# Where the taps of a 31-wide depthwise convolution add up: SBUF tiles or one PSUM bank

## What is computed

```python
z = u @ w_in                                   # q, six k/v sets, gates, conv input, merge gates
kc = compress(kv[0], ...); vc = compress(kv[1], ...)
#   compress: 31 overlapping windows of 32 tokens -> gelu(flat @ w1) @ w2
o_c, o_s, o_w = nsa_attention(q, kc, vc, ...)  # 8 heads of 64, query blocks of 128

c = c_val * sigmoid(c_gate)                    # 512 channels
c = causal_dwconv(c, conv_w, conv_b)           # 31 taps per channel, 512 tokens
c = silu(layernorm(c)) ; y_b = c @ w_conv_out + b
h = h + (sigmoid(..) * y_a + sigmoid(..) * y_b) @ w_out
```

## Time and profile before

| | |
|---|---|
| median of three runs | 2301.78 us |
| profiled execution | 2300.76 us, of which the span of the trace is 2298.8 us |
| TensorE matmul busy | 2156.7 us (94%) |
| VectorE busy | 1082.4 us (47%) |
| ScalarE busy | 863.0 us (38%) |
| GpSimd busy | 925.4 us (40%), 855.4 of it `w_lo` |
| mean granted TensorE clock | 0.973 of full speed |
| the tap instruction, SBUF accumulator | 90 times, 104.0 us |
| the tap instruction, PSUM accumulator | 29 times, 21.7 us |

### The profile page before, as it was taken

One profiled execution on the slowest core, in us unless ns is written; L12 is line 12 of the kernel. 1 busy time (PEld: TensorE's weight loads), 2 busy tenths in 40 slices (PEclk: granted clock), 3 DMA queues, 4 the chain that ended last, 5 costly groups with the idle time before them and its releaser, 6 DMA issues.

```text
span 2298.8 us, 25188 instructions
## 1 busy us (share of the span) xinstructions
PE 2156.7 (94%) x10138; PEld 1766.7 (77%) x10138; DVE 1082.4 (47%) x1665; ACT 863.0 (38%) x1344; POOL 925.4 (40%) x415
## 2 busy tenths in 40 slices
PE   7449999999999999989999999999899999999996
PEld 6437777778888888777777888888788788888875
DVE  3996666535552423556654423222553245222145
ACT  4123444434442335444443423223532234233243
POOL 4242222344444444522215444443654454444452
PEclk9779999999999999999999999999999999999998
DMA  4122111223333233211112233232223223333321
GB/s 151 55 92 65 47 45 48 73 92 102 101 92 101 93 105 105 64 56 56 46 37 93 92 101 101 92 101 92 93 71 103 90 75 101 93 100 97 96 90 49
DMA packets 53252, 192.73 MB, mean 84 GB/s; under 512 B 5904, under 2 KB 6032, under 8 KB 53136
## 3 DMA queue, kind: packets, MB, share of 16 engines
q1 hardware_dynamic: 52704, 189.55, 26.4%
q10 hardware_dynamic: 432, 1.57, 0.2%
HBM read 189.00 MB, written 2.10 MB: 83 GB/s over the span
## 4 chain that ended last, share of the span: by engine, by line
PE 82%; DVE 12%; ACT 5%; issue 1%; POOL 0%; DMA 0%; DVEq 0%; ACTq 0%; POOLq 0%
PE ps L461 25%; PE ps L463 24%; PE ps L462 24%; DVE conv_acc L1044 4%; PE ps L625 1%; PE ps L605 1%; PE ps L864 1%; ACT w_hi L1646 1%; DVE ps L1553 1%; PE ps L617 1%; PE ps L524 1%; PE ps L882 1%; DVE resid L1558 1%; DVE tile_a L1312 1%; PE ps L517 1%
## 5 line engine op out<-in xcount | busy, mean ns | idle before, releaser
L425 POOL TENSOR_TENSOR w_lo<-w_raw,w_hi 128x1024 fp32r<-128x1024 f32 x353 | 855.4, 2425 | 1303.8 <-ACT w_hi L1646 1303.8
L461 PE MATMUL ps<-xg_hi,w_hi 128*128 128x512 f32 x1776 | 712.1, 401 | 38.1 <-POOL w_lo L425 17.1
L463 PE MATMUL ps<-xg_hi,w_lo 128*128 128x512 f32 x1776 | 697.2, 393 | 0.0
L462 PE MATMUL ps<-xg_lo,w_hi 128*128 128x512 f32 x1776 | 697.0, 392 | 0.0
L1646 ACT ACTIVATE w_hi<-w_raw 128x1024 fp32r<-128x1024 f32 x353 | 372.7, 1057 | 623.6 <-PE ps L463 615.0
L461 PEld LDWEIGHTS ps<-xg_hi,w_hi 128*128 128x128 f32 x1776 | 336.8, 190 | 107.6 <-issue 22.2
L463 PEld LDWEIGHTS ps<-xg_hi,w_lo 128*128 128x128 f32 x1776 | 336.2, 189 | 71.7
L462 PEld LDWEIGHTS ps<-xg_lo,w_hi 128*128 128x128 f32 x1776 | 337.2, 190 | 63.9 <-issue 0.2
L462 PE MATMUL ps<-h_lo,w_hi 128*128 128x512 f32 x688 | 267.9, 389 | 0.0
L463 PE MATMUL ps<-h_hi,w_lo 128*128 128x512 f32 x688 | 267.9, 389 | 0.0
L461 PE MATMUL ps<-h_hi,w_hi 128*128 128x512 f32 x688 | 267.9, 389 | 0.0
(11 more groups left out here) (303 smaller groups left out, 2335.2 us busy)
## 6 DMA issues: line engine op xcount, KB each, us to landing
w_raw<-in_weights SPq DMA_DIRECT2D x353, 512.0 KB, 3.5
resid<-in_x SPq DMA_DIRECT2D x4, 512.0 KB, 6.9
out_x<-resid SPq DMA_DIRECT2D x8, 256.0 KB, 2.0
p_raw<-in_p ACTq DMA_DIRECT2D x3, 512.0 KB, 3.6
vec<-in_vectors SPq DMA_DIRECT2D x1, 252.5 KB, 4.3
```

Of the source, the lines that this page charges most:

```text
L425: pool.tensor_tensor(w_lo[:, slot, :], w_raw[:, u % RAW, :], w_hi[:, slot, :].bitcast(F32), ALU.subtract).then_inc(w_ready, 1)
L461: pe.matmul(o, w, x, start=start, stop=False)
L462: pe.matmul(o, w, xl, start=False, stop=False)
L463: return pe.matmul(o, wl, x, start=False, stop=stop)
```

## The change

All four channel tiles now add up in bank 7, one after the other; the last tap of each writes the finished sum to `conv_acc[:, ct, :]`, as tile 3's did. Since the next tile's first tap overwrites the bank, it waits for the last tap of the tile before it. Bank 7 is therefore taken from the first tap on, and both kinds of compressed features are turned into bank 6: kind 0 into columns 0 to 127, kind 1 into columns 128 to 255. TensorE may not write kind 1 while VectorE or ScalarE still read kind 0 there, so `hidden_turn(1)` waits for `hidden_low(0)`.

```diff
             def hidden_turn(kv):
                 pe.wait_ge(s_cmp["gelu"], kv + 1)
+                if kv:
+                    pe.wait_ge(s_cmp["glo"], 1)
                 for half in range(2):
-                    mm = pe.transpose(ps[:, 6 + kv, half * 64:half * 64 + 2 * NC1], ...)
+                    mm = pe.transpose(ps[:, 6, kv * P + half * 64:kv * P + half * 64 + 2 * NC1], ...)
...
                     ct, k = divmod(n, CONV_TAPS)
-                    acc, src, w = conv_acc[:, ct, :], glu[:, ct, k:k + S], vcol("conv_w", n)
-                    if ct == CT - 1:
-                        acc = ps[:, NB, :]
+                    acc, src, w = ps[:, NB, :], glu[:, ct, k:k + S], vcol("conv_w", n)
                     if k == 0:
+                        if n:
+                            dve.wait_ge(s_mrg["conv"], n)
                         ins = dve.tensor_scalar(acc, src, w, vcol("conv_b", ct), ALU.mult, ALU.add)
```

More of the change, by code:

```diff
@@ L550, in hidden_turn @@
                 pe.wait_ge(s_cmp["gelu"], kv + 1)
+                if kv:
+                    pe.wait_ge(s_cmp["glo"], 1)
                 for half in range(2):
-                    mm = pe.transpose(ps[:, 6 + kv, half * 64:half * 64 + 2 * NC1], hid[:, kv, half * P:(half + 1) * P],
+                    mm = pe.transpose(ps[:, 6, kv * P + half * 64:kv * P + half * 64 + 2 * NC1], hid[:, kv, half * P:(half + 1) * P],
                                       ident[0:2 * NC1, 0:2 * NC1])
@@ L1088, in hidden_low @@
                 dve.wait_ge(s_cmp["ghi"], kv + 1)
-                low(hid_lo[:, kv], ps[:, 6 + kv, 0:P].rearrange("p (a b) -> p a b", b=64)[:, :, 0:2 * NC1], hid_hi[:, kv],
+                low(hid_lo[:, kv], ps[:, 6, kv * P:(kv + 1) * P].rearrange("p (a b) -> p a b", b=64)[:, :, 0:2 * NC1], hid_hi[:, kv],
                     s_cmp["glo"])
@@ L1710, in hidden_high @@
                 act.wait_ge(s_cmp["turned"], kv + 1)
-                copy_hi(hid_hi[:, kv], ps[:, 6 + kv, 0:P].rearrange("p (a b) -> p a b", b=64)[:, :, 0:2 * NC1], s_cmp["ghi"])
+                copy_hi(hid_hi[:, kv], ps[:, 6, kv * P:(kv + 1) * P].rearrange("p (a b) -> p a b", b=64)[:, :, 0:2 * NC1], s_cmp["ghi"])
             def keys(j):
```

## The result

| | before | after |
|---|---|---|
| median | 2301.82 us (4 runs, 2301.23 to 2309.78) | 2274.28 us (4 runs, 2272.36 to 2276.49) |
| profiled execution | 2300.76 us | 2272.36 us |
| its span | 2298.8 us | 2270.6 us |

The ratio is 0.9873, 95% interval 0.9849 to 0.9896. The kernel is 27.5 us faster; 33.0 were forecast (2268.8 us, range 2264 to 2275). The time is inside the range, near its slow end.

What follows compares the result with a forecast made beforehand. VectorE's taps were taken to bound the kernel from 52.3 to 170.3 us, TensorE after that. VectorE's 32.5 us plus 0.5 us from TensorE's clock made 33.0 us, so 2301.8 becomes 2268.8 us, range 2264 to 2275.

Steps and rivals of the forecast that it cites:

- A: Dependent taps in PSUM are slower than isolated ones, up to 21 us over 80 taps: 2272 to 2290 us; 4%.
- B: Compression chain becomes the bound at `hidden_low(0)`, `values` 0 comes 3 to 7 us later: 2272 to 2276 us; 5%.
- the cycle table: 120 fixed cycles for a PSUM source, 58 for SBUF: 65 ns more a tap, 5.2 us over 80, 2274 us.
- The stall: Taps with one PSUM operand no longer wait for `w_lo`: 16 long taps on the path save 32.3 us.
- The sum of VectorE's stretch: From 52.3 to 170.3 us VectorE saves 32.5 us, so `values` 0 starts at about 137.8.
- First taps: Three on the path become 804 ns: one saves 0.7 us, two cost 0.26 us each; together 0.2 us saved.
- Spacing in PSUM: Dependent taps keep SBUF's 0.787 us; bounds 0.01 us less a tap and 0.04 us more (3.2 us).
- D: Each tap reads back the PSUM value just written; at 0.5 us extra a tap, 2308.8 us; 2%.
- The slack list: Competitors for the path stay early enough: 2.3 us of slack at `hidden_low(0)`, 6 us at `keys` 1.
- The new wait: `hidden_turn(1)` waits for `hidden_low(0)`, asked for at 118.5, TensorE there at 123 to 125 us: costs nothing.
- TensorE's clock: Half speed at `values` 0 cost 1.7 us; 0.5 us gain taken; attention's start may move 1 us either way.

Runs made afterwards that it cites:

- Experiment 2: Kernel before, with `w_lo` cut to 8 of 1024 columns for units 7 to 24, which leaves work out: 2270.56 us, ratio 0.9858.
- experiment 9: Changed kernel, but channel tile 0 (taps 0 to 30) adds up in SBUF as before: 2284.73 us, ratio 0.9922.
- experiment 1: Kernel before, with only the features turned into bank 6 and the new wait of `hidden_turn(1)`; taps stay in SBUF: 2301.84 us, ratio 0.9997.
- experiment 6: Changed kernel with taps moved from ahead of `keys` 1 to around the `values` units and into the attention: 2268.76 us, ratio 0.9845.
- experiment 7: Changed kernel with taps moved around the `values` units and into the attention, plus 34 idle TensorE matmuls: 2266.35 us, ratio 0.9832.
- experiment 8: Kernel before, accumulators of tiles 0 to 2 in SBUF, with taps moved around the `values` units and into the attention: 2302.88 us, ratio 0.9993.
- 11: Changed kernel with ten taps moved to where VectorE waits behind `keys` 1, plus all 34 idle matmuls: 2261.94 us, ratio 0.9819.
- 12: Changed kernel with ten taps moved to VectorE's waits behind `keys` 1, plus only the 10 idle matmuls ahead of the attention: 2262.79 us, ratio 0.9827.
- 3, changed again: The changed kernel run once more, unaltered: 2274.61 us, ratio 0.9878.
- experiment 10: Changed kernel with ten taps moved from between the `cmp_in` units to where VectorE waits behind `keys` 1: 2263.97 us, ratio 0.9831.
- 5, idle at `cmp_out`: Changed kernel with only the 24 idle TensorE matmuls around `cmp_out`: 2273.15 us, ratio 0.9856.
- experiment 4: Changed kernel with 34 idle TensorE matmuls, ahead of and behind `cmp_out` and ahead of the attention: 2267.14 us, ratio 0.984.

## Why the prediction was right, and what it missed

**The time.** The measured 2274.28 us lies 5.5 us above the forecast, outside the 3 us that the prediction gave to spacing, clock and run. It is inside the range only because that was stretched to 2275 for the near parts of rivals A and B, and neither happened. That part is luck. The total alone would fit A, B and the 2274 us of the cycle table as well; it is the trace that separates them.

**The stall.** Right. The taps with two SBUF inputs waited for `w_lo`; with one input in PSUM they do not. Experiment 2 removes the other party of the collision and gets the same stretch, experiment 9 brings back one tile and gets its share.

**The sum of VectorE's stretch.** 32.5 us forecast, 32.44 measured. It came from counting long taps on the chain of waits, not from the group's mean: the whole group of 90 also holds two long taps behind `keys` 1, which would have added 4 us that TensorE hides. That it fits to 0.1 us is closer than the terms are known.

**First taps.** 804 ns forecast, 811 measured. **Spacing in PSUM.** 0.787 us forecast; 7.08 us for nine gives 0.79. Rivals A and D had nothing in them. The estimate of 65 ns a tap from the cycle table of the Trainium skill (VectorE: DVE Perf Modes, the section on the TRN2 errata) is not borne out either, although its total of 2274 us is what was measured: 80 taps dearer by 65 ns would have made VectorE's stretch 5.2 us longer, and it came out as forecast.

**The slack list.** `hid_hi(0)` came at 116.3 and VectorE at 119.5, 3.0 us later, against 2.3 forecast. The new wait cost nothing in the changed kernel, and nothing in the median of experiment 1, where it was long. Rival B did not occur.

**TensorE's clock.** This is the step that failed: "I take 0.5 us from between 0 and 1.7", and "1 us either way" at the attention's start. Measured were -1.36 and -1.66 us. The bounds left no room for a loss at the `values` units. The clock still fell, at about 134.7 us, at the end of TensorE's wait of 4.2 us ahead of `cmp_out`, and it was at half speed for 6 us of `values` 0 instead of 3. Here are the same stretches in nine of the fourteen traces, with the time at half speed in us, first from the start of `values` 0 on, then at the attention's start (read from the clock of 4 us stretches), and all that lies behind the score maximum. Experiments 6 to 8, 11 and 12 are left out: they move taps into the attention or combine two changes, and do not compare one to one (11 takes 23.67 us from `keys` 1 to `q0` with none at half speed).

| kernel | glu 0 to `keys` 1 | `keys` 1 to `q0` | `q0` to score max. | at half speed | behind it |
|---|---|---|---|---|---|
| before | 128.58 | 24.27 | 21.20 | 2.9, 6.8 | 2083.9 |
| 1, bank and wait alone | 128.51 | 25.65 | 22.88 | 5.9, 10.2 | 2083.9 |
| 2, small `w_lo` | 95.25 | 24.24 | 21.17 | 2.9, 6.9 | 2087.3 |
| changed | 96.14 | 25.63 | 22.86 | 5.8, 10.2 | 2083.8 |
| 3, changed again | 96.17 | 25.17 | 22.88 | 4.8, 10.2 | 2086.8 |
| 9, tile 0 in SBUF | 109.08 | 24.35 | 21.29 | 3.1, 6.8 | 2084.0 |
| 10, taps placed | 88.39 | 24.32 | 21.24 | 3.0, 6.8 | 2084.0 |
| 5, idle at `cmp_out` | 96.16 | 22.88 | 22.87 | 0, 10.2 | 2089.8 |
| 4, idle at both | 96.20 | 22.89 | 18.28 | 0, 0 | 2089.7 |

The two later stretches follow the time at half speed in every row, and experiments 4 and 5 take it away by themselves. So the clock as the cause of the two losses is shown. Why the changed kernel has the longer times at half speed is not. A shorter stage or a shorter gap is not enough for it: experiments 2, 9 and 10 have both and lose nothing, and experiment 10 has the same wait of 4.2 us ahead of `cmp_out`. Experiment 1, with VectorE's stretch of before, has both losses. Each of these kernels but the changed one has one trace only, so what belongs to the kernel and what to the execution stays open.

The missing 5.5 us of the median are these 3.5 us, 1.3 us of late start in the profiled execution, which is scatter, and 0.9 us by which the profiled execution of after lies farther below its median than that of before (1.9 against 1.1 us); 0.2 us less outside the span goes the other way. The 3.5 us are 1.86 at the `values` units, where 0.5 had been counted as a gain, and 1.66 at the attention's start.

## What to carry to other kernels

When an instruction has a median of 0.75 us and a maximum of 2.9, look at both ends, not at the mean: here the long ones each stand beside one instruction of another engine, and a change of operand from SBUF to PSUM removes them. Count on the chain of waits how many of them are on the path. When a stage shrinks, write down the TensorE gaps that remain and price the work behind each at half clock too, as a range with a loss in it. Compare kernels by stretches between milestones and not by totals alone: two losses to half speed, about 3 us together, came and went from kernel to kernel and hid in the totals of experiments 2, 9 and 10. Place the work that you move in the stretches where its engine waits (experiment 10); moved into the attention it made that stage over 15 us longer (experiments 6 and 8).

## What the runs showed of the hardware

- The collision costs both sides: a VectorE instruction of 0.76 us took 2.78, and a `w_lo` of 2.40 us took 2.74 on average when they alternated.
- It also catches one-input instructions from SBUF to SBUF. The first tap as `tensor_scalar`, 536 ns alone, took 1542 as the first one before, and the `tensor_scalar` of the probabilities took at most 547 ns in the changed kernel and up to 2558 in experiment 6. Beside instructions with two SBUF inputs the Trainium skill names those in a two-port mode (GPSIMD Engine Reference, Specifications). That this form runs in such a mode no run here shows directly; the trace agrees in that it is stretched beside `w_lo`, while with its output in PSUM it takes 803 to 814 ns each time.
- One operand in PSUM ends the stall for the tap: 120 of 120 at most 756 ns, with GpSimd at `w_lo` beside many of them.
- TensorE's granted clock fell at the end of a wait of 4.2 us. It was back at full speed at about 145 us, 6 us after `values` 0 began, with TensorE busy all that time; in the kernel before and in experiments 2, 9 and 10 it was back after 3 us.
- In the attention the clock dips for some us in every trace, at 304 to 312 us in the profile after and at 204 to 212 in that of experiment 4. In the two traces of the changed kernel what lies behind the score maximum differs by 2.9 us (2083.8 and 2086.8), while the clock of their 8 us stretches adds up to 62 and 69 us at half speed there.
